# Delta-rule inversion with half-width moving operands: products of 64 instead of 128 columns at each doubling level

## The reference

```python
lower = jnp.where(strict, jnp.einsum('bnhid,bnhjd->bnhij', kb, kc) * decay, 0.0)
eye = jnp.eye(CHUNK, dtype=lower.dtype)
rhs = jnp.concatenate([vc * bc[..., None], kb * jnp.exp(gc)[..., None]], axis=-1)
sol = lax.linalg.triangular_solve(lower + eye, rhs, left_side=True, lower=True,
                                  unit_diagonal=True)
```

## Time and profile before

| | before |
|---|---|
| median of 3 runs, us | 2566.03 |
| lowest and highest, us | 2562.74, 2566.20 |
| the profiled execution, us | 2567.36 |
| its span, first to last instruction, us | 2565.4 |
| mean granted clock of TensorE in it | 0.989 |
| PE busy | 2486.9 us, 97% |
| PE weight loads busy | 2298.4 us, 90% |
| DVE busy | 1704.4 us, 66% |
| ACT busy | 1226.1 us, 48% |
| HBM over the span | 166 GB/s |

### The profile page before, as it was taken

One profiled execution on the slowest core, in us unless ns is written; L12 is line 12 of the kernel. 1 busy time (PEld: TensorE's weight loads), 2 busy tenths in 40 slices (PEclk: granted clock), 3 DMA queues, 4 the chain that ended last, 5 costly groups with the idle time before them and its releaser, 6 DMA issues.

```text
span 2565.4 us, 39119 instructions
## 1 busy us (share of the span) xinstructions
PE 2486.9 (97%) x17068; PEld 2298.4 (90%) x17068; DVE 1704.4 (66%) x1856; ACT 1226.1 (48%) x1277; POOL 0.2 (0%) x4
## 2 busy tenths in 40 slices
PE   7999999999999998999999999999899999999997
PEld 6999898789998996899989999878799899998876
DVE  5699866656898666665646557566567657577674
ACT  5445226463552255543343433346546555455573
POOL 0000000000000000000000000000000000000000
PEclk9999999999999999999999999999999999999999
DMA  5454223464442233555455555555344545555553
GB/s 210 162 182 147 97 97 112 156 223 156 177 155 102 94 124 130 204 182 187 182 185 186 188 182 184 193 213 186 147 179 173 191 181 181 181 181 180 182 196 115
DMA packets 63211, 428.48 MB, mean 167 GB/s; under 512 B 6976, under 2 KB 7104, under 8 KB 13504
## 3 DMA queue, kind: packets, MB, share of 16 engines
q1 hardware_dynamic: 60496, 414.97, 45.1%
q10 hardware_dynamic: 2544, 11.01, 1.2%
HBM read 421.76 MB, written 4.19 MB: 166 GB/s over the span
## 4 chain that ended last, share of the span: by engine, by line
PE 87%; DVE 7%; ACT 4%; issue 2%; DMA 0%; DVEq 0%; SPq 0%; ACTq 0%
PE PS L407 86%; DVE Q L1472 2%; ACT Q L884 2%; DVE QA L1476 1%; PE PS L497 1%; DVE WL L1507 1%; DVE X L1476 1%; ACT WH L898 1%; DVE Q L1476 0%; ACT QA L884 0%; DVE Y L1472 0%; DVE SM L1491 0%; ACT L884 0%; PE PS L698 0%; ACT HH L884 0%
## 5 line engine op out<-in xcount | busy, mean ns | idle before, releaser
L1507 DVE TENSOR_TENSOR WL<-W,WH 128x2048 fp32r<-128x2048 f32 (+2 forms) x388 | 861.1, 2223 | 534.0 <-ACT WH L898 533.2
L898 ACT ACTIVATE WH<-W 128x2048 fp32r<-128x2048 f32 (+2 forms) x388 | 717.3, 1858 | 738.7 <-PE PS L407 608.0
L407 PE MATMUL PS<-HH,WL 128*128 128x256 f32 x3392 | 563.9, 286 | 16.7 <-DVE WL L1507 12.1
L407 PE MATMUL PS<-HH,WH 128*128 128x256 f32 x3392 | 557.2, 284 | 0.0
L407 PE MATMUL PS<-HL,WH 128*128 128x256 f32 x3392 | 556.9, 284 | 0.0
L407 PEld LDWEIGHTS PS<-HH,WL 128*128 128x128 f32 x3392 | 473.9, 193 | 23.9 <-DVE WL L1507 12.7
L407 PEld LDWEIGHTS PS<-HH,WH 128*128 128x128 f32 x3392 | 472.8, 193 | 0.0
L407 PEld LDWEIGHTS PS<-HL,WH 128*128 128x128 f32 x3392 | 472.4, 192 | 0.0
L407 PE MATMUL PS<-WL,HH 128*128 128x512 f32 (+2 forms) x768 | 228.2, 378 | 13.3 <-DVE HL L1472 13.3
L407 PE MATMUL PS<-WH,HL 128*128 128x512 f32 (+2 forms) x768 | 222.5, 370 | 0.0
L407 PE MATMUL PS<-WH,HH 128*128 128x512 f32 (+2 forms) x768 | 221.8, 369 | 0.0
(11 more groups left out here) (134 smaller groups left out, 1963.8 us busy)
## 6 DMA issues: line engine op xcount, KB each, us to landing
W<-in_wall SPq DMA_DIRECT2D x378, 1024.0 KB, 4.8
W<-in_wall SPq DMA_DIRECT2D x16, 512.0 KB, 3.5
W<-in_wall SPq DMA_DIRECT2D x8, 536.0 KB, 3.3
X<-in_x SPq DMA_DIRECT2D x4, 512.0 KB, 8.3
X<-in_x ACTq DMA_DIRECT2D x1, 2048.0 KB, 10.0
xsave<-X ACTq DMA_DIRECT2D x1, 2048.0 KB, 8.6
X<-xsave ACTq DMA_DIRECT2D x1, 2048.0 KB, 10.1
Q<-in_g_post ACTq DMA_DIRECT2D x8, 256.0 KB, 3.4
```

Source lines behind the costliest of these rows:

```text
L407: return e.matmul(o, l, r, start=start, stop=stop, skip_group_check=True)
L898: e.activation(WH[:, s % NSPL, 0:m], W[:, c % NRAW, 0:m], ACT.Copy).then_inc(*up("hi", c))
L1507: e.tensor_tensor(WL[:, c % NRAW, 0:m], W[:, c % NRAW, 0:m], WH[:, s % NSPL, 0:m].bitcast(F32), ALU.subtract).then_inc(*up("lo", c))
```

## The change

At every level from m = 8 on, the x product takes as moving operand only the columns of the first half of each block of TT_: 64 columns in 128/m runs of m/2, read with a step of m. The u product takes the second halves of UU, the t product the first halves of XX, at all levels. The products of the four units of a bank are stored side by side in 256 columns. The stationary operands stay whole.

VectorE reads 256 columns out of each bank instead of 512 and writes to the same halves of XX, UU and TT_. XX's second halves are no longer overwritten with zeros, so the u product has wrong values in some rows; its update becomes a scalar_tensor_tensor that multiplies the product with a new table column `first{m}` (1 for rows in the first half of a block, 0 otherwise) and adds. At m = 4 the x products and masks stay as they are. The number of instructions on every engine, their order, the waits and the rests are the same.

```diff
+        c[f"first{m}"] = (i % m < m // 2)[:, None]
...
+        def half(ap, m, k):
+
+            return ap.rearrange("p (b s c) -> p b s c", s=2, c=m // 2)[:, :, k, :]
...
-                            i = mm(b[:, 128 * j:128 * j + 128], DS[:, us], TT_[:, us], start=(j == 0))
+                            if m == 4:
+                                i = mm(b[:, 128 * j:128 * j + 128], DS[:, us], TT_[:, us], start=(j == 0))
+                            else:
+                                i = mm(b[:, 64 * j:64 * j + 64], DS[:, us], half(TT_[:, us], m, 0), start=(j == 0))
...
-                                l_, r_ = (XX, UU) if which == "u" else (UU, XX)
-                                i = mm(b[:, 128 * j:128 * j + 128], l_[:, us], r_[:, us], start=(j == 0))
+                                l_, r_, s = (XX, UU, 1) if which == "u" else (UU, XX, 0)
+                                i = mm(b[:, 64 * j:64 * j + 64], l_[:, us], half(r_[:, us], m, s), start=(j == 0))
...
-                        tt(quad(XX[:, cs]), quad(sbank("dn", l, "x", m, k)),
-                           tbl(f"lv{m}").unsqueeze(1).to_broadcast([128, 4, 128]), ALU.mult, "dn_v", l, "x", m, k)
+                        lv = tbl(f"lv{m}").unsqueeze(1).to_broadcast([128, 4, 128])
+                        if m == 4:
+                            tt(quad(XX[:, cs]), quad(sbank("dn", l, "x", m, k)), lv, ALU.mult, "dn_v", l, "x", m, k)
+                        else:
+                            x4, v4 = (v.rearrange("p u (b c) -> p u b c", c=m)[:, :, :, 0:m // 2]
+                                      for v in (quad(XX[:, cs]), lv))
+                            p4 = sbank("dn", l, "x", m, k)[:, 0:256].rearrange("p (u b c) -> p u b c", u=4, c=m // 2)
+                            tt(x4, p4, v4, ALU.mult, "dn_v", l, "x", m, k)
...
-                        tt(UU[:, cs], UU[:, cs], sbank("dn", l, "u", m, k), ALU.add, "dn_v", l, "u", m, k)
+                        pu, pt = (sbank("dn", l, x_, m, k)[:, 0:256].rearrange("p (b c) -> p b c", c=m // 2)
+                                  if x_ == "u" or m < 128 else None for x_ in "ut")
+                        uh = half(UU[:, cs], m, 1)
+                        stt(uh, pu, tb(f"first{m}"), uh, ALU.mult, ALU.add, "dn_v", l, "u", m, k)
                         if m < 128:
-                            tt(TT_[:, cs], TT_[:, cs], sbank("dn", l, "t", m, k), ALU.add, "dn_v", l, "t", m, k)
+                            th = half(TT_[:, cs], m, 0)
+                            tt(th, th, pt, ALU.add, "dn_v", l, "t", m, k)
```

## The result

The changed kernel takes 2570.3 us in the median of 9 runs (2567.91 to 2572.45), the kernel before 2566.03 in as many taken beside it. The ratio of the means is 1.0021, with a 95% interval of 1.0011 to 1.0031: slower by 4.3 us between the medians and 5.3 us between the means. That is about the 0.2% (5.1 us) up to which I had counted a difference as none, and clear of the noise. The profiled execution of the changed kernel (2567.91 us, as the fastest of its runs) shows nearly nothing of it: its span is 0.5 us longer than that of before. What it does show is what the change makes of the work itself.

The account below looks back on a forecast made before the run. TensorE, busy 97% of the span, was taken as the bound. From 2567.36 us profiled, PE 0 and bank waits -0.2 gave 2567.2; that execution stood 1.3 us above the median, hence 2565.8 us, range 2559 to 2572.

Parts of the forecast that it names:

- the forecast that nothing changes beyond a measurement's noise: Whole kernel: PE's pace unchanged, median 2565.8 us, within 0.2% (5.1 us) of before; chance 80%.
- The step on which I let everything rest: Inversion bursts on PE: loading 128 weight columns sets the pace, so 64-column records still take 112 ns; change 0 us.
- rival A: Narrowed products: the moving stream sets the pace, a 64-column record takes 54 ns; gain 45 us, 2521 us; 7%.
- B: Narrowed products: load and stream hinder each other, so pairs drop from 112 to about 100 ns; gain 9 us, 2557 us; 5%.
- One reading on the way: PE's bursts: the second record stands about 30 ns behind the first, so time between groups is divided by records less one.
- A saving of 23.1 us: VectorE in both layers: 256-column masks and adds cut its busy time, but beside PE, so hardly any time is gained.
- the bursts' edges: PE's inversion bursts: 768 records at an unchanged pace, PE's term 0 us.
- The 0.2 us that I took off for bank waits: First u/t burst of each layer, level 4: shorter VectorE adds close a 0.10 us bank wait; -0.2 us in all.
- Rival C: Level-4 u and t products: strided reads at a quarter rate make records take 216 ns; 10 us slower, 2576 us; 5%.
- rival D: Long 48-record bursts: PE's clock falls, about 1.7 us each; one for each of ten gives 17 us, 2583 us; 3%.
- the window from 77 to 89 us: Row of narrow matmuls where the clock stays at 1.00; cited against the clock falling in narrow bursts.
- the fall of the earlier trace, at 387.4 us: Granted clock 0.50 for 3.4 us after PE had idled 2.1 us; each such stretch priced at about 1.7 us.

Follow-up runs that it names:

- after_later: Changed kernel with the level-4 u and t products and their additions one step later; median 2564.18 us, ratio 0.9997 to the kernel before.
- before_later: Kernel before, all products 128 wide, with the level-4 u and t products and their additions one step later; 2563.40 us, ratio 0.9993.
- level4_contiguous: Changed kernel with level-4 u and t moving operands as 64 columns side by side, their results dropped; 2570.63 us, ratio 1.0020.
- before_again: The kernel before, unchanged, timed once more against itself; median 2564.40 us, ratio 0.9996.
- table_only: Kernel before with only the six new table columns added, shifting tables and tiles; 2564.78 us, ratio 0.9998.
- dve_alone: Against the changed kernel: TensorE's products as before, VectorE reads only the needed halves out of 512-column banks; 2566.19 us, ratio 1.0003.
- level4_wide: Changed kernel with level-4 u and t products and VectorE's level-4 additions as before, later levels narrow; 2566.78 us, ratio 1.0005.

## Why the prediction was wrong

The time of 2570.3 us lies 4.5 us above the 2565.8 that were forecast and inside the range of 2559 to 2572. What failed is the forecast that nothing changes beyond a measurement's noise, and its reason: that the clock would stay as it was.

**Right: the pace.** The step on which I let everything rest held. Bursts kept 112 ns a record with 64 columns, with gaps of every width, and their loads took as long as before; rivals A and B are out. One reading on the way was wrong and did no harm: the second record of a burst starts 108 ns behind the first, not 30 (before, at 304.52 and at 309.93 us); the successor's 30 ns alone make it right to divide by one record less. The Trainium skill's rule in "TensorE: Matmul & The Clock Gate", section "LDWEIGHTS (loading the stationary operand)", agrees in that the columns of the weights set the time of a record (112 ns measured here, an estimated 107 by the rule).

One sum is off by a little: by the rule that rival A takes from the Trainium skill's section "Back-to-back issue gap" ("TensorE: Matmul & The Clock Gate"), two passes of 64 columns are an estimated 58 ns and not 56, since its 2.5 ns count twice; nothing hangs on it.

**Right: VectorE.** A saving of 23.1 us was forecast, 22.7 came, and it bought nothing.

**Right in mechanism, mis-sized: the bursts' edges.** From the first level-8 record to the first record behind the inversion the first layer takes 72.06 us instead of 71.73, 0.3 us more, where I had 0; this fits the 0.0004 by which after_later stands above before_later (their intervals overlap). The 0.2 us that I took off for bank waits did not come: the level-4 burst takes 5.38 us to its successor in both kernels, 0.1 more than the later ones, so that tenth is not a wait that shorter additions close.

**Rival C** (the strided read) is out by level4_contiguous, which reads without gaps and loses as much.

**The step that failed: rival D and what I took for its counter-evidence.** I gave the clock 3%, asked only whether a long narrow burst as such could make it fall, and answered with the window from 77 to 89 us, where narrow matmuls run at clock 1.00. That answer was even right: 72 narrow records in a row hold the clock. But no idle time stands ahead of that window. The one burst to be narrowed that does have idle time ahead stood in my own rows, with 1.35 us; I looked at that wait only as a cost that remains, not as a circumstance that the narrow burst would follow. And the falls last 10.2 us there, not the 3.4 of the earlier trace rows: 5.1 us each, not 1.7, so that one in an execution is enough for 0.2%. The sum had no term for the clock; the 5.3 us between the means are about one such fall in an execution, an estimate, since only profiled executions show their falls. Nor is the fall of the earlier trace rows, at 387.4 us, a fixed cost: of the five profiles with the level-4 burst of before in its old place and full-width products (before, before_again, table_only, dve_alone, level4_wide) one alone has it.

**What stays open.** Shown is that at level 4 the half width and the idle time ahead are both needed for these falls and that they make the loss, and that the places of the tables, the gaps and VectorE's new operations are not needed. Not shown is that level 4 itself is: a narrow level-8 burst behind 1.46 us kept its clock, but at another moment relative to the possible changes of the clock. Why the six level-4 bursts all had theirs at 1.8 to 2.3 us is open too. The level-4 wait is that long only in executions without a fall shortly before it: with one at 270 us PE comes 1.7 us later and the wait shrinks (in before_again, with such a fall, to 0.2 us in the second layer). That this picks the executions in which the moment fits is argued, not shown.

No version here beats the kernel before clearly. The best is before_later, full width with the level-4 step moved: 2563.4 us, 0.9993 with an interval up to 1.0002.

## What to carry to other kernels

Look at which half of a load-and-matmul pair sets the pace before halving the other: with 128 weight columns an fp32 record takes 112 ns with 12, with 64 and with 128 moving columns, so halving them saves nothing, and to gain here the loads would have to go. Making a stream thinner isn't free where the pace stays the same: look at each place where the thin burst follows idle time of TensorE, and price a fall of the clock there by the longest one that you can find, with the times and the mean clock of several runs and not one profile as the judge. And move the consumer of a late mask by a step before anything else; that alone took away all that the change had lost (0.9997).

## What the runs showed that I had not expected

- The granted clock fell to 0.50 while PE was busy in every microsecond, 1.8 to 2.3 us into a burst of 64-column products behind 1.3 us of idle time, and stayed there for 10.2 us, although full-width projection matmuls followed from 8.5 us on.
- 1.46 us of idle time and the same kind of burst at level 8 did not do that, in six bursts, all with the possible change of the clock within 0.5 us of their start instead of some 2 us behind it; nor did full-width bursts behind 1.3 to 1.8 us.
- Idle time that was added ahead of full-width bursts cost about twice its length. Most of the rest is a fall of 3.4 us at a later wait of 2.10 us, behind each inversion; the same wait had a fall behind 17 of 18 inversions that were held up and behind 2 of 22 others.
- The profiled execution was the fastest of nine runs and had none of the level-4 falls; a single execution's mean clock can be off by 0.002 through a stretch at its start that costs no time.
